# Prompt attention in a decoder trunk on one core: the weighted sum issued ahead of the scores in each row block's turn

## What is computed

```python
def fox_attend(q, k, v, cq, ck, q_pos, k_pos):
    s = jnp.einsum('bqhd,bkhd->bhqk', q, k) * (1.0 / math.sqrt(HEAD_DIM))
    decay = transpose(cq)[..., :, None] - transpose(ck)[..., None, :]
    mask = k_pos[None, :] <= q_pos[:, None]
    s = jnp.where(mask[None, None], s + decay, -jnp.inf)
    p = jax.nn.softmax(s, axis=-1)
    return jnp.einsum('bhqk,bkhd->bqhd', p.astype(v.dtype), v)
```

## Time and profile before

| what | value |
|---|---|
| median of 3 runs | 2330.48 us (2330.12 to 2331.57) |
| the profiled execution: its own time | 2329.15 us |
| its span | 2327.3 us |
| granted TensorE clock, mean | 0.995 |
| PE busy | 2282.0 us (98%) |
| DVE busy | 1031.1 us (44%) |
| ACT busy | 576.9 us (25%) |
| POOL busy | 613.1 us (26%) |
| prompt attention, from its first scores to the first matmul behind it | 1208.15 to 1485.05 us of the span |

### The profile page before, as it was taken

How to read it: one execution, slowest core, us unless ns; L and a number is a source line. 1 busy time by engine, 2 the same in 40 slices (tenths; PEclk the granted TensorE clock), 3 DMA queues, 4 the chain that set the end, 5 groups by cost and what they waited for, 6 DMA issues and landing times.

```text
span 2327.3 us, 36318 instructions
## 1 busy us (share of the span) xinstructions
PE 2282.0 (98%) x14220; PEld 2092.5 (90%) x14220; DVE 1031.1 (44%) x1755; ACT 576.9 (25%) x1264; POOL 613.1 (26%) x439
## 2 busy tenths in 40 slices
PE   7999999999999999999989999999999999999999
PEld 7999999999999967777766666899999999999999
DVE  7842332433323756442136777534433423324332
ACT  5420110110101433332126666422100101101101
POOL 6122222222233612100000110353222222222240
PEclk9999999999999999999989999999999999999999
DMA  4111111111111124444554544111111111111112
GB/s 151 32 50 51 46 46 46 46 46 46 46 46 46 59 74 152 139 133 147 177 165 97 133 114 110 32 46 45 46 49 50 48 47 46 46 46 46 46 55 75
DMA packets 195560, 169.96 MB, mean 73 GB/s; under 512 B 28784, under 2 KB 169120, under 8 KB 195399
## 3 DMA queue, kind: packets, MB, share of 16 engines
q1 hardware_dynamic: 155657, 142.03, 20.8%
q10 hardware_dynamic: 39750, 25.69, 3.6%
HBM read 137.55 MB, written 30.50 MB: 72 GB/s over the span
## 4 chain that ended last, share of the span: by engine, by line
PE 90%; DVE 7%; issue 2%; ACT 1%; DMA 0%; SPq 0%; DVEq 0%; ACTq 0%
PE ps L363 35%; PE ps L616 28%; PE ps L791 13%; PE ps L1490 2%; PE ps L1514 2%; PE ps L490 2%; DVE stat L1576 2%; PE ps L1476 1%; PE ps L1475 1%; PE ps L1265 1%; PE ps L1290 1%; ACT pT L1560 1%; PE ps L807 1%; PE ps L1755 1%; PE ps L1245 1%
## 5 line engine op out<-in xcount | busy, mean ns | idle before, releaser
L363 PE MATMUL ps<-xn_hi,w_lo 128*128 128x352 f32 x1536 | 497.1, 324 | 5.0 <-DVE h L690 3.2
L363 PE MATMUL ps<-xn_lo,w_hi 128*128 128x352 f32 x1536 | 492.4, 321 | 0.0
L363 PE MATMUL ps<-xn_hi,w_hi 128*128 128x352 f32 x1536 | 492.3, 321 | 0.0
L616 PE MATMUL ps<-hid_hi,w_lo 128*128 128x352 f32 x1440 | 464.5, 323 | 0.0
L616 PE MATMUL ps<-hid_lo,w_hi 128*128 128x352 f32 x1440 | 461.9, 321 | 0.0
L616 PE MATMUL ps<-hid_hi,w_hi 128*128 128x352 f32 x1440 | 461.4, 320 | 0.0
L330 POOL CAST w_hi<-w_raw 128x1024 fp32r<-128x1024 f32 x132 | 139.0, 1053 | 1003.4 <-issue 516.7
L690 DVE TENSOR_TENSOR h<-ps,h 128x352 f32<-128x352 f32 x360 | 185.6, 521 | 413.3 <-PE ps L616 413.3
L655 ACT ACTIVATE tmp_b<-tmp_a 128x352 f32<-128x352 f32 x192 | 95.1, 499 | 1092.1 <-DVE tmp_a L673 1092.1
L332 POOL TENSOR_TENSOR w_lo<-w_raw,w_hi 128x1024 fp32r<-128x1024 f32 x132 | 318.8, 2415 | 10.6
L363 PEld LDWEIGHTS ps<-xn_hi,w_lo 128*128 128x128 f32 x1536 | 288.1, 188 | 7.3 <-DVE h L690 4.3
(11 more groups left out here) (243 smaller groups left out, 2729.9 us busy)
## 6 DMA issues: line engine op xcount, KB each, us to landing
w_raw<-in_w_up SPq DMA_DIRECT2D x64, 512.0 KB, 3.9
w_raw<-in_w_down SPq DMA_DIRECT2D x60, 512.0 KB, 3.3
out<-tok_out ACTq DMA_DIRECT2D x32, 256.0 KB, 2.1
qk_dram<-turn_hi ACTq DMA_DIRECT2D x32, 256.0 KB, 2.4
qk_dram<-turn_lo ACTq DMA_DIRECT2D x32, 256.0 KB, 2.9
k_page<-in_cache_k SPq DMA_DIRECT2D x32, 256.0 KB, 3.2
v_page<-in_cache_v SPq DMA_DIRECT2D x16, 512.0 KB, 9.5
q_a<-qk_dram SPq DMA_DIRECT2D x32, 256.0 KB
```

The source lines that it names most:

```text
L363: last = pe.matmul(ps[:, bank, 0:CH], w, x(k, c), start=(k == 0 and i == 0), stop=(k == nk - 1 and i == 2))
L616: last = pe.matmul(ps[:, NC * (dm % 2) + c, 0:CH], w, x, start=(k == 0 and i == 0), stop=(k == GT - 1 and i == 2))
```

## The change

In each turn PE issues the weighted sum's two key blocks directly behind the transposes, and the scores of block n + 3 behind those. Every instruction, wait and tile stays the same, as do the queues of all other engines. In turns 6 and 7 of each head, which have no weighted sum, and in turns 0 to 3 of the first head, PE's order stays as it was.

```diff
             for n in range(NBLK):
                 turn(n)
-                if n + 3 < NBLK:
-                    score(n + 3)
                 if n % NQ in (4, 5):
                     weigh(n - n % 4 - 1, 2 * (n % 4))
                 elif n % NQ < 4 and n >= NQ:
                     weigh(n - n % 4 - 1, 2 * (n % 4))
+                if n + 3 < NBLK:
+                    score(n + 3)
                 if n == 14:
                     pe.wait_ge(o_ev, 6)
                     weigh_sample(pe, 2, O_BANK[2])
```

## The result

The changed kernel takes 2352.35 us (median, 2351.54 to 2353.31) against 2330.72 us before: a ratio of 1.0093, 95% interval 1.0081 to 1.0105, or 21.6 us more. The two profiled executions differ by 22.4 us (2351.54 against 2329.15). 21.4 of these lie in the stage of the change: it ran from 1208.15 to 1485.05 us before and runs from 1208.93 to 1507.21 now. The other 1.0 us is spread ahead of it (0.8) and behind it (0.2). The profile before also has a loss that the profile after has not: from 1213 to 1216 us, in head 0, its granted clock is 0.50. From the first scores to turn 4 of head 0, where both kernels issue the same, it takes 8.73 us and the changed kernel 7.69. Without that 1.0 us the stage has grown by 22.4.

The account below looks back on a forecast made before the run. PE was taken as the bound, paced in turns 4 and 5 by a ring through DVE and ACT. Turn 0's 4.6, turns 1 to 3's 3.6 and turns 4 and 5's 16.6 us gave +24.8 on 2329.15: 2354.0, range 2341 to 2360.

Parts of the forecast that it names:

- a ring that starts at the scores: Turns 4 and 5: block 7's scores, DVE's maximum, ACT's exponential and copies, then PE's turn 6, each waiting for the last.
- Turns 4 and 5: +1.04: Per head in us: 0.94 from block 7's late scores delaying turn 6, plus 0.1 in turn 4 from a late copy.
- Turns 1 to 3 have a turn of slack: Blocks 0 to 3 have one quad each, so later scores cost only the joints, 0.08 us a turn.
- The maximum of block 7 has 0.29 us of slack on DVE: In turn 4, 0.29 us between block 7's mask matmul ending and its maximum starting absorbs part of the scores' delay.
- The scores and sum of turn 5 lie in PE's wait and cost nothing: Turn 5's reordered work falls within the wait ahead of turn 6, so its joints add nothing.
- Turn 6 waits 1.2 us or so for ACT: Sign in the profile after: turn 6's transposes wait about 1.2 us for ACT's copy in place of 0.53.
- Turn 0: a wait of 0.24 us: In 14 heads the first sum waits for ACT's copies of turn 7, formerly hidden by scores: +0.24 us.
- The joints: +0.08 a turn: Switching between transposes, sum and scores in the new order costs +0.08 us a turn, between -0.03 and +0.15.
- the unseen one: The joint from the sum to the scores, which no profile row showed; taken as +0.03 us.
- Rival 1: DVE and ACT catch up and only the joints remain: +7.3 us, 2336.5, chance 0.08.
- rival 2: Joints gain 0.21 us a turn, 91 times, and the ring doesn't bind: -19 us, 2310, chance 0.03.
- theory B: Experiments' theory: the ring has other entrances, above all block 6's scores in turn 3, because DVE's queue passes delay to block 7.

Follow-up runs that it names:

- turn 4 alone: Kernel before, with the weighted sum ahead of the scores in turn 4 of each head only: 2350.72 us, ratio 1.0088.
- turn 3 alone: Kernel before, with the weighted sum ahead of the scores in turn 3 of each head only: 2343.93 us, ratio 1.006.
- maximum first: Kernel before, PE's order kept, with DVE's maximum of block 7 ahead of its two output copies in turn 4: 2341.8 us, ratio 1.0047.
- scores-first kernel: Kernel before, with every turn issuing scores, then transposes, then the sum: 2322.61 us, ratio 0.9967.
- The kernel with one edit more: Scores first in turns 0 and 4, maxima first in turns 4 and 6, plus the sum ahead of transposes in turn 1: 2322.89 us, ratio 0.9965.
- the best single turn: Kernel before, with the scores ahead of the transposes in turn 0 only: 2325.31 us, ratio 0.9978.

## Why the prediction was right, and where it was not

The time, the sign and the main cause hold: 2354.0 was forecast, 2352.35 measured. That the two are so close is partly luck: the growth was forecast with 24.8 us and measured with 21.6, and half of the difference is made good by the profiled execution it was added to, which lies 1.6 us below the median before. Point by point:

- *PE's waits come from a ring that starts at the scores.* Shown. Turn 6 follows the start of block 7's maximum: in head 5 it is 1.09 later where the maximum is 1.10 later (turn 4 alone), 0.88 where it is 0.89 (turn 3 alone), and 0.13 earlier where it is 0.13 earlier (maximum first). The one exception among the rows above is head 4 with the maximum first, where the norm of block 6 comes last.
- *Turns 4 and 5: +1.04.* Measured +0.98 in the mean, but divided otherwise. In the even head that was read it is 0.89: the ring's 0.94 held within 0.05, and the 0.1 did not come on top of it. In odd heads it is 1.04, because they had less slack. Turn 4 grew by 0.33 instead of 0.10, and turn 5 by 0.65 instead of 0.94. The stop is ahead of turn 5: its transposes start 0.36 us after the mask matmul (1299.83 to 1300.19), where 0.07 is usual, and for the like stop of turn 3 alone the profile names ACT's copies. Since turn 6 is set by the ring, what turn 4 takes turn 5 gives back.
- *Turns 1 to 3 have a turn of slack, so they cost their joints.* This is the step that failed, although its sum held (+0.06 each, forecast +0.08). The argument looked at the transposes that a turn does (blocks 1 to 3, one quad each) and not at the scores that it issues: turn 3 issues those of block 6. Alone, turn 3 costs 13.3 us. In the change it adds little only because turn 4's late scores bring nearly the same delay.
- *The maximum of block 7 has 0.29 us of slack on DVE.* It is so in even heads only: block 7's mask matmul ends as early in odd heads, and the maximum there starts 0.13 us sooner. And it is there only while DVE is on time. With block 6 late, DVE's queue is what the maximum waits for. So the sign that was named, that this maximum now waits for PE, came only in odd heads, with 0.19 us, and in none of the even ones.
- *The scores and sum of turn 5 lie in PE's wait and cost nothing.* Right in the change, where turn 7 kept its length. Alone they cost 6.5 us, through DVE's queue.
- *Turn 6 waits 1.2 us or so for ACT.* The profile has 0.92 and 0.94. The rest stands ahead of turn 5, where some 0.3 us of stop (0.36 less the usual 0.07) was not forecast.
- *Turn 0: a wait of 0.24 us.* It was about 0.15. The sum starts 0.05 us behind the end of ACT's copies (1305.43 + 1.07 = 1306.50, to 1306.55), and not 0.14 as the transposes do.
- *The joints: +0.08 a turn.* Measured +0.06, with the unseen one near what was taken: from sum to scores it is 1.02 us (1297.78 to 1298.80), the same as from sum to transposes, and the first score matmul bears 0.50 us instead of 0.48, so 0.02 where 0.03 was put. By the rule on changes of tiling mode in the Trainium skill's TensorEngine Tiling (Array Packing), Key Properties, it would be nothing, and the whole +20 us. The trace agrees that entry to and exit from the sum cost something: five transposes take 0.64 us up to the sum (1297.14 to 1297.78) and 0.52 up to scores, and two transposes 0.19 behind a sum and 0.15 behind a mask matmul. But the old order's three joints and the new order's differ by 0.06 us, so they are not all alike.
- *Rival 1*, PE covers everything (+7), and *rival 2* (-19) fell with the result. The scores-first kernel has the change's joints and is faster.

What stays open: theory B's sizes lie within 2 us of what was measured in eight kernels, are off by 3 for turn 4 alone (+17 against +20.1), and by 5 to 8 in the three in which DVE's order is changed. The place between heads 14 and 15, which no theory had, explains the 3, and some 2.6 of the 5 with the maximum first. The theory has the ring's entrances right, and DVE's side of it only roughly.

## What to carry to other kernels

When an instruction is moved in one engine's queue, look at what it feeds and not at the work of the turn in which it stands: the scores moved in turn 3 were those of the block that sets turns 5 and 6. In a ring of in-order queues, several late starts end in the same wait, so that undoing one edit gives back 1 us of 20, and the costs of the edits one by one add to about twice the whole; only undoing several together shows what they share. And before single heads are compared, see whether they alternate: two heads next to each other differed here by 0.13 us, as much as one of the effects looked for. Work that depends on nothing late belongs ahead of a wait: placing the scores before the transposes in three of eight turns was worth 0.43% over the kernel before, with not one instruction changed.

## What the runs showed of the hardware that was not expected

TensorE's granted clock fell to 0.50 (1.2 instead of 2.4 GHz) for some microseconds inside stages in which PE is nearly full, and not always after the same waits.

In the kernel with scores first in turns 0 and 4 and maxima first, a PE wait of 1.42 us, from 1238.83 to 1240.25, was followed by six microseconds at a granted clock of 0.50, with PE busy without a break. The stretch with the wait in it, 1236 to 1242, has PE busy for 4.58 of 6.00 us. The kernel with one edit more has the same wait, the same 4.58 us and a clock of 0.57 behind it. The kernel with turn 4 alone has waits of 1.43 us in its heads, and its clock stayed at 1.00 from 1300 to 1470 us, as it did in the change with its 0.92 us. Only behind the wait of 1.90 us in head 14 did it fall, to 0.50 from 1486 to 1488. In head 0, the kernel before and the changed kernel issue the same and have the same waits, 1.12 and then 0.36 or 0.37 us; the clock was 0.50 from 1213 to 1216 us in the one and 1.00 in the other. So the length of the wait before it did not decide it in these runs, and they don't tell what did.

What a fall cost can be read from the kernels that had none: 1.0 us in head 0 of the kernel before. Between heads 1 and 2, with the maxima first, the 4.0 us lost are the wait of 1.42 us and some 2.6 of the clock, half of what the best single turn wins (5.2).

The other surprise is the norm of 128 columns that took 2.07 us instead of 0.29 while POOL's subtraction (L332) ran beside it. In the kernel before, a norm of 384 columns beside the same subtraction took 1.73 us (at 1466.65) instead of 0.42, and cost nothing, because PE was not waiting for it.
